# A diffusion block's seam from the residual to the feed-forward: order of the last tile's work, and two weight parts on another engine

## The reference

```python
def rms_norm(x, g):
    y = xf * lax.rsqrt(jnp.mean(xf * xf, axis=-1, keepdims=True) + EPS)
    return (y * g.astype(jnp.float32)).astype(x.dtype)
def modulate(x, g, shift, scale):
    return rms_norm(x, g) * (1 + scale) + shift
def swiglu(h, w_in, w_out):
    gate, up = jnp.split(h @ w_in, 2, axis=-1)
    return (jax.nn.silu(gate) * up) @ w_out
...
        mix = merge_branches(ya, yb, yc, gate, w_branch[l], w_out[l])
        x = x + mod_x[2] * rms_norm(mix, norm_g[l, 1])
        h2 = modulate(x, norm_g[l, 2], mod_x[3], mod_x[4])
        x = x + mod_x[5] * rms_norm(swiglu(h2, w_ffn_in[l], w_ffn_out[l]), norm_g[l, 3])
```

## Time and profile before

| | us |
|---|---|
| median of 3 runs (lowest to highest) | 1778.95 (1778.5 to 1782.03) |
| profiled execution, its own time | 1780.69 |
| its span in the trace | 1778.9 |
| PE busy in the span | 1740.1 (98%) |
| DVE busy | 1220.4 (69%) |
| ACT busy | 807.2 (45%) |
| POOL busy | 763.2 (43%) |

### The profile page before, as it was taken

How to read it: one execution, slowest core, us unless ns; L and a number is a source line. 1 busy time by engine, 2 the same in 40 slices (tenths; PEclk the granted TensorE clock), 3 DMA queues, 4 the chain that set the end, 5 groups by cost and what they waited for, 6 DMA issues and landing times. The chain is left out here.

```text
span 1778.9 us, 25756 instructions
## 1 busy us (share of the span) xinstructions
PE 1740.1 (98%) x9180; PEld 1481.9 (83%) x9180; DVE 1220.4 (69%) x1719; ACT 807.2 (45%) x1580; POOL 763.2 (43%) x490
## 2 busy tenths in 40 slices
PE   8999999999998999999999999999999999999998
PEld 6997888888887999899988878778888888888886
DVE  3529588889958999778833366875566566575766
ACT  3525333344646888656620145643333333344453
POOL 0316677776533899430022242365555555400000
PEclk9999999999998999999999999999999999999999
DMA  8333333444767655512034242223223323386734
GB/s 309 119 103 113 131 119 125 159 167 174 266 179 209 170 135 139 159 32 72 1 142 160 89 166 84 83 98 127 94 94 124 124 94 125 117 277 204 257 103 177
DMA packets 98375, 249.86 MB, mean 140 GB/s; under 512 B 12257, under 2 KB 25953, under 8 KB 98146
## 3 DMA queue, kind: packets, MB, share of 16 engines
q1 hardware_dynamic: 98274, 248.52, 41.8%
HBM read 183.07 MB, written 65.41 MB: 140 GB/s over the span
## 5 line engine op out<-in xcount | busy, mean ns | idle before, releaser
L729 POOL TENSOR_TENSOR ring<-raw_w,ring 128x512 fp32r<-128x512 f32 x120 | 186.8, 1575 | 139.3 <-ACT ring L600 139.2
L78 PE MATMUL psum<-h_hi,ring 128*128 128x512 f32 x400 | 156.3, 391 | 2.6 <-ACT z L646 2.0
L80 PE MATMUL psum<-h_hi,ring 128*128 128x512 f32 x400 | 156.3, 391 | 0.0
L79 PE MATMUL psum<-h_lo,ring 128*128 128x512 f32 x400 | 156.3, 391 | 0.0
L78 PE MATMUL psum<-u_slot 128*128 128x512 f32 x308 | 120.4, 391 | 0.8 <-DVE u_slot L2927 0.7
L80 PE MATMUL psum<-u_slot 128*128 128x512 f32 x308 | 120.2, 390 | 0.0
L79 PE MATMUL psum<-u_slot 128*128 128x512 f32 x308 | 119.9, 389 | 0.0
L600 ACT ACTIVATE ring<-raw_w 128x512 fp32r<-128x512 f32 x120 | 72.6, 625 | 99.5 <-DVE raw_w L889 31.0
L1380 DVE TENSOR_REDUCE mx<-psum 128x1 f32<-128x1280 f32 x64 | 95.2, 1487 | 8.6 <-PE psum L1266 7.5
L1313 ACT ACTIVATE e<-psum,neg_m 128x1280 f32<-128x1280 f32 x64 | 85.0, 1329 | 31.9 <-DVE neg_m L1381 31.9
L2526 POOL TENSOR_TENSOR cut_lo<-i_raw,cut_hi 128x512 fp32r<-128x512 f32 x44 | 66.9, 1520 | 59.2 <-ACT cut_hi L2381 59.2
(11 more groups left out here) (411 smaller groups left out, 5221.5 us busy)
## 6 DMA issues: line engine op xcount, KB each, us to landing
raw_w<-in_w_pairs SPq DMA_DIRECT2D x40, 512.0 KB, 4.5
qk_dram<-room SPq DMA_DIRECT2D x26, 512.0 KB, 3.6
room<-in_w_ada SPq DMA_DIRECT2D x24, 512.0 KB, 5.1
gates_dram<-ost SPq DMA_DIRECT2D x24, 512.0 KB, 3.0
b_g<-gates_dram SPq DMA_DIRECT2D x8, 1536.0 KB, 7.6
stage<-in_w_ff SPq DMA_DIRECT2D x22, 512.0 KB, 5.9
i_raw<-in_w_ff SPq DMA_DIRECT2D x22, 512.0 KB, 4.8
f_dram<-h SPq DMA_DIRECT2D x22, 512.0 KB, 3.4
```

The lines of the kernel that those rows point to most:

```text
L78: pe.matmul(out, sh, mh, start=first, stop=False, skip_group_check=onto)
L79: pe.matmul(out, sh, ml, start=False, stop=False, skip_group_check=onto)
L80: return pe.matmul(out, sl, mh, start=False, stop=last, skip_group_check=onto)
L729: pool.tensor_tensor(w_lo[i], source(p, i), w_hi[i].bitcast(F32), ALU.subtract).then_inc(w_lo_ready, 1)
```

## The change

Five moves, all in residual_ffn_in. (1) The low parts of weights 6 and 1 of step 0 go from DVE to POOL, ahead of POOL's low parts of tile 5; the semaphore w0_lo becomes two, one for each engine. (2) For the last tile DVE multiplies acc by row before it waits for the root, frees PSUM then, and applies root and addition to x in one scalar_tensor_tensor. (3) ACT copies t1 before tile 6's modulations instead of after five of them. (4) The last tile's chain: ACT runs all modulations of tile 6 and its four of tile 7 before t1_hi(6); DVE runs its four, and both sums, before part_lower(6, 0), with semaphores of their own (last_full, last_sums); part_lower(7, 0) goes ahead of part_lower(6, 1), and product(1,0) waits for six low parts instead of seven. (5) POOL makes the low part of product(0,1)'s weight before the half sums of tile 6 instead of after. The number of instructions that compute stays the same.

```diff
@@ block.tensor
-            pe.wait_ge(w0_lo, w0_at(1))
-            pe.wait_ge(part_lo, 2 * FH - 1)
+            pe.wait_ge(*w0_lo_of[1])
+            pe.wait_ge(part_lo, 2 * FH - 2)
...
-            pe.wait_ge(full_ready, KC * TL)
+            pe.wait_ge(full_ready, KC * LAST + KC // 2)
+            pe.wait_ge(last_full, KC // 2)
@@ block.scalar
             first_weight_hi(5)
-            modulate(LAST - 1, 0, 5)
             act.wait_ge(prod0, prod0_at(0))
             act.wait_ge(taken, TL)
             act.activation(t1, banks[0], ACT.Copy).then_inc(t1_ready, 1)
             square_x(LAST)
             act.sem_inc(fw_hi_ready, PRODUCTS)
             weight_hi(1, 1, 0)
-            modulate(LAST - 1, 5, KC)
+            modulate(LAST - 1)
+            modulate(LAST, 0, KC // 2)
             t1_hi(LAST - 1)
...
-            modulate(LAST, 0, KC // 2)
             t1_hi(LAST)
@@ block.gpsimd
-                if t == LAST - 1:
-                    pool.sem_inc(fw_lo_ready, PRODUCTS)
-                    weight_lo(1, 1, 0)
...
             half_sums(FH + 1)
-            pool.wait_ge(w0_lo, 3)
+            pool.wait_ge(chunk_done, 4)
+            for i in W0[:2]:
+                pool.wait_ge(w0_hi, w0_at(i))
+                pool.tensor_tensor(f_lo[i], source(0, i), f_hi[i].bitcast(F32), ALU.subtract).then_inc(w0_lo_pool, 1)
...
+            pool.sem_inc(fw_lo_ready, PRODUCTS)
+            weight_lo(1, 1, 0)
             half_sums(FH + 2)
@@ block.vector
+                if t:
+                    v.wait_ge(turned, t)
+                if t == LAST:
+                    ch.link(v.tensor_tensor(xn[:], acc, row[:], ALU.mult))
+                    v.sem_inc(taken, 1)
                 v.wait_ge(root_ready, 2 * t + 1)
                 ch.link(v.reciprocal(root(0), root(0)))
...
+                if t == LAST:
+                    v.scalar_tensor_tensor(out=x[t % 2][:], in0=xn[:], scalar=root(0), in1=x[t % 2][:], op0=ALU.mult,
+                                           op1=ALU.add).then_inc(x_ready, 1)
...
                     v.wait_ge(chunk_done, 4)
-                    for i in W0[:3]:
-                        first_weight_lo(i)
+                    first_weight_lo(2)
...
-            v.wait_ge(part_lo, 4)
-            part_lower(LAST - 1, 0)
             v.wait_ge(turned, TL)
             for k in range(KC // 2, KC):
                 v.tensor_scalar(h2[:, k, LAST * P:TL * P], turned_x(LAST, k), A2[:, k:k + 1], B2[:, k:k + 1], ALU.mult,
-                                ALU.add).then_inc(full_ready, 1)
+                                ALU.add).then_inc(last_full, 1)
...
+            v.wait_ge(part_lo, 4)
+            part_lower(LAST - 1, 0)
+            part_lower(LAST, 0)
             part_lower(LAST - 1, 1)
-            part_lower(LAST, 0)
             part_lower(LAST, 1)
```

More of the change, by code:

```diff
@@ L2113, in residual_ffn_in @@
             sem(f"fi_{n}") for n in ("w_hi", "w_lo", "s", "acc", "t1", "p5", "z", "u2", "x", "silu", "f", "dve"))
-        w0_hi, w0_lo, prod0 = sem("fi_w0_hi"), sem("fi_w0_lo"), sem("fi_acc0")
+        w0_hi, w0_lo_pool, w0_lo_dve, prod0 = sem("fi_w0_hi"), sem("fi_w0_lo_pool"), sem("fi_w0_lo_dve"), sem("fi_acc0")
+        last_full, last_sums = sem("fi_last_full"), sem("fi_last_sums")
         W0 = (6, 1, 2, 4, 5)
@@ L2117, in residual_ffn_in @@
         w0_at = lambda i: W0.index(i) + 1
+        w0_lo_of = {6: (w0_lo_pool, 1), 1: (w0_lo_pool, 2), 2: (w0_lo_dve, 1), 4: (w0_lo_dve, 2), 5: (w0_lo_dve, 3)}
         prod0_at = lambda i: ORDER0.index(i) + 1
@@ L2195, in step @@
                     sp.wait_ge(m_lo_ready, TL + 1)
-                    sp.wait_ge(w0_lo, len(W0))
+                    sp.wait_ge(w0_lo_pool, 2)
+                    sp.wait_ge(w0_lo_dve, 3)
                 for j in range(2):
@@ L2358, in t1_hi @@
                     act.wait_ge(m_lo_ready, TL)
-                act.wait_ge(sums_done, 2 * (t - FH) + 1)
+                if t == LAST:
+                    act.wait_ge(last_sums, 1)
+                else:
+                    act.wait_ge(sums_done, 2 * (t - FH) + 1)
                 act.activation(t1_part[0][:, :, first_half(t)], h2[:, 0:KH, first_half(t)], ACT.Copy).then_inc(part_hi, 1)
             def t3_hi(t):
-                act.wait_ge(sums_done, 2 * (t - FH) + 2)
+                if t == LAST:
+                    act.wait_ge(last_sums, 2)
+                else:
+                    act.wait_ge(sums_done, 2 * (t - FH) + 2)
                 act.activation(t3_part[0][:, :, first_half(t)], h2[:, 0:KH, second_half(t)], ACT.Copy).then_inc(part_hi, 1)
@@ L2606, in s13 @@
                 if q == 1:
-                    v.wait_ge(w0_lo, w0_at(2))
+                    v.wait_ge(w0_lo_pool, 2)
+                    v.wait_ge(*w0_lo_of[2])
                 elif q:
@@ L2645, in _ @@
                 v.tensor_scalar(ss[:, t % 2, 0:1], ss[:, t % 2, 0:1], 1.0 / D, EPS, ALU.mult, ALU.add).then_inc(mean_ready, 1)
+                if t:
+                    v.wait_ge(turned, t)
+                if t == LAST:
+                    ch.link(v.tensor_tensor(xn[:], acc, row[:], ALU.mult))
+                    v.sem_inc(taken, 1)
                 v.wait_ge(root_ready, 2 * t + 1)
                 ch.link(v.reciprocal(root(0), root(0)))
[L2648 to L2652, removed]
                 v.wait_ge(x_in[t % 2], 16 * (t // 2 + 1))
-                v.tensor_tensor(x[t % 2][:], x[t % 2][:], xn[:], ALU.add).then_inc(x_ready, 1)
+                if t == LAST:
+                    v.scalar_tensor_tensor(out=x[t % 2][:], in0=xn[:], scalar=root(0), in1=x[t % 2][:], op0=ALU.mult,
+                                           op1=ALU.add).then_inc(x_ready, 1)
+                else:
+                    ch.link(v.scalar_tensor_tensor(out=xn[:], in0=acc, scalar=root(0), in1=row[:], op0=ALU.mult, op1=ALU.mult))
+                    v.sem_inc(taken, 1)
+                    v.tensor_tensor(x[t % 2][:], x[t % 2][:], xn[:], ALU.add).then_inc(x_ready, 1)
                 if t == LAST:
```

22 lines of the change are left out of this document (11 added, 11 removed).

## The result

The changed kernel takes **1782.2 us** (median; 1779.8 to 1785.2), the kernel before, measured beside it on the same chips, 1780.0 (1777.1 to 1783.5). The ratio is **1.0012, with a 95% interval of 1.0007 to 1.0018**: 2.2 us longer, less than the 0.2% that counts as a difference here, and on the slow side. The profiled execution took 1781.96 us with a span of 1780.0; PE is busy for 1737.0 us of it, DVE 1220.2, ACT 807.1 and POOL 767.8.

What follows compares the result with a forecast made beforehand. The seam was taken as bound by DVE's queue from the last tile's sums on. POOL's turns and the new order sum to +1.6 us there, giving 1778.95 + 1.6 = 1780.6 us, range 1777.5 to 1782.5.

Steps and rivals of the forecast that it cites:

- DVE and POOL take turns: At the last tile's weight sums, POOL's two new low parts alternate with DVE; the mean comes 1.75 us later.
- The rival in which POOL relieves DVE: POOL's low parts fit beside DVE's weight sums without delaying them; product(1,0) 1.4 us earlier, time 1778.15; chance 0.19.
- The t1 copy: ACT's copy after product(0,0) begins at 1131.65, +0.2 us, so the first gap stays about 2.2 us.
- The fused add: DVE's last-tile scalar_tensor_tensor meets POOL's second sum and ends at 1133.75, +1.35 us.
- the half-rate rival: The fused add runs at half throughput, +2.8 us, 1781.7; chance 0.06, shared with any other loss of 2.2 to 3.5.
- xn and product(0,1): Normalised last tile finished at 1136.3, +0.5 us; product(0,1) starts at 1138.8, −0.45, waiting for ACT instead of POOL.
- The new order on DVE: Last tile's second sum ends at 1142.7, product(1,0) starts at 1144.0 (+0.95 us), four low parts end at 1145.1 (+1.6).
- The clock in product(1,0): A clock drop after the gap of about 2.2 us adds 1.6 to PE's 0.95; later gaps absorb it, about +1.8.
- Behind this DVE runs the same queue without a hole: After the last tile's low parts, DVE's queue stays rigid, so all later work through product(1,1) is 1.6 us later.
- less hides behind DVE: A clock loss decides the time only from 3 us on, 6.3 us at half clock; smaller losses stay hidden.
- The clock rival: After the gap before product(1,0), half clock lasts 10.30 us instead of 3.4; +3.5 us, 1782.5; chance 0.08.
- The seam closes: All three first gaps vanish and DVE's queue follows, winning over half of 6.7 us, 1775 or less; chance 0.05.

Runs made afterwards that it cites:

- e2: Kernel before with only the low parts of weights 6 and 1 moved from DVE to POOL: 1781.9 us, ratio 1.0006.
- e1: Changed kernel with the low parts of weights 6 and 1 back on DVE: 1781.33 us, ratio 1.0007 against the kernel before.
- e7: e5 and e6 together, plus DVE's first two weight sums of step 1 between the low parts of B22: 1776.97 us, ratio 0.998.
- e3: Changed kernel with eight unread matmuls in PE's gap before product(1,0): 1782.28 us, ratio 1.0008 against the kernel before.
- e8: Changed kernel with the t1 copy back behind five modulations of tile 6: 1783.94 us, ratio 1.0014 against the kernel before.
- e6: Kernel before with ACT's t1 and z copies earlier in step 1 and DVE's z sum ahead of the next weights' sums: 1777.26 us, ratio 0.9982.
- e10: e7 with eight unread matmuls in the gap before product(3,0): 1778.24 us, ratio 0.9987 against the kernel before.
- e5: e1 with the t1 copy and POOL's low part for product(0,1) back in their old places: 1780.27 us, ratio 0.9993 against the kernel before.

## Why the prediction was right, point by point

- **DVE and POOL take turns: right**, and the main term. The mean was put at 1130.2 and came at 1130.23. e2 has the same rows without any of the other edits, e1 the other edits without the rows. The rival in which POOL relieves DVE falls with the rows of 1.60 and 1.65 us.
- **The t1 copy: right.** Put at 1131.65, it began at 1131.65 (1130.38 and 1.27).
- **The fused add: right.** Put to end at 1133.75, it ended at 1133.76; it lost one turn to POOL and took 1.91. Where no POOL turn comes before it, it takes 1.28 (e1, and e7 too). With that the half-rate rival falls. What the Trainium skill (Vector Engine (DVE) Microarchitecture Reference, Points that are easy to get wrong) says of this form with two such sources, half throughput, does not hold for it here: 1.28 us, against 1.21 to 1.23 for other instructions of 1024 columns; the measurement decides.
- **xn and product(0,1): right.** xn ends at 1136.36 (put at 1136.3), product(0,1) starts at 1138.88 (put at 1138.8) and waits for ACT.
- **The new order on DVE: right.** The second sum was put to end at 1142.7 and ends at 1142.77; product(1,0), put at 1144.0, starts at 1144.08; the four low parts end at 1145.17 (put at 1145.1).
- **The clock in product(1,0): the mechanism right, the term mis-sized.** The text saw that the drop could come after a gap of about 2 us and priced it at "about +1.8" in all, since "the gaps of 0.30, 0.72 and 1.29 take that up". Product(1,1) came at 1159.97, 2.61 later than before, instead of 1159.0. Of the three gaps only one gave anything, 0.72 to 0.16. The 0.30 stayed because it is PE's wait for its own product, not slack behind POOL; the 1.29 stayed because the queue that ends it had become later too. The step that failed is "Behind this DVE runs the same queue without a hole": its z sum waits for product(2,0), 0.26 us in after and nothing in e3. So a loss of 1.6 us does not hide behind DVE, as "less hides behind DVE" has it. With the clock kept the sum holds: product(1,1) comes 43.57 us after the eighth tile, 1158.92 on the prediction's clock, and the seam is +1.66, the 1.6 of the sum; with the drop it is +2.09.
- **The clock rival (+3.5): not in this kernel.** The half clock lasted 3.4 us, not 10. But "it costs little in either kernel, since turn(7) there waits for other engines anyway" is not what the rows show: before, turn(7) began at 1136.60, right behind product(3,0), 0.8 us after the normalised tile it reads was ready (1135.79). The drop was cheap because nobody waited for turn(7): DVE was busy with part_lower(6, 0) until 1138.08. The change's own order takes that work away from there. In e8 the half clock lay over all of product(3,0), DVE waited for turn(7) behind it, and the seam was 1.0 longer than the change's.
- **The seam closes: no.** It would have needed DVE's queue 3.6 us earlier, and it came 1.65 to 2.05 later. e6 shows the same from the other side: a gain came as soon as what PE waits for in step 1 was moved ahead in ACT's and DVE's order. The "6.7 us" as "all that the change can win" was also a little small, since each gap that went in e6 was worth about 0.24 us more than its idle time.
- **The time.** 1780.6 was forecast and 1782.2 measured. Of the 1.6 us between them, 1.05 is the kernel before itself (1778.95 from three runs, 1780.0 from the 22 beside the change); the forecast difference was 1.65, the measured one is 2.2, and most of the rest is the 0.43 of the clock. The seam's +2.09 lies inside the forecast's +0.9 to +2.2, near its upper end. That the time lies in its range as well, by 0.3 us, is partly luck: the range was laid around a median that was 1.05 too low. The times alone, whose interval reaches 1 us to each side here, don't tell +1.6 from +2.1.

## What to carry to other kernels

Before work is moved from DVE to GpSimd, look for rows of the two engines whose ends interlock: where they take turns on SBUF operands, an instruction moved out of a dependent chain can lengthen the chain by more than its own time (here 1.28 us given away, and the chain 1.79 later). Find the queue on which the last gaps hang, and shorten it or move ahead in it what the bottleneck engine waits for: three gaps in front of it were traded for one another without any gain, while a few copies and one sum moved within the step behind them gave 2.5 us. And when a stretch at half clock is priced, follow who reads the results of the slowed matmuls, not only whether PE has a gap later that could take up the loss.

## What the runs showed of the hardware that was not expected

- **The same starts can give the turn to either engine, and a turn is worth more than 1 us.** Counted from the eighth tile, the fused adds of e7 and e10 start at 14.71 and 14.72 us, beside POOL instructions that start at 13.31 in both, and their durations differ by 1.15 us. What decided the turn is not shown. A sum worked out turn by turn is no better than that at such a place.
- **The length of a gap doesn't tell whether the clock falls.** After 2.05 us of idle time before product(3,0) the granted clock was 0.62 in the kernel before and 0.64 in e7, but 1.00 in e5; after 2.20 us it was 1.00 before product(3,0) in the change and half before product(1,0) of the same run. Nor does it tell for how long: around a gap of 3.85 us the clock was half for some 6.7 us in e8 (0.79 over the 3.88 us up to product(3,0), 0.62 over the 6.72 from it on), over all of product(3,0), and after 3.86 us in e2 some 3.4 us (0.64 over 4.67 us). What decides between gaps of the same length was not settled.
